# Five attentions of a two-block model: the mask's addition moved from TensorE to VectorE, the division by the sum from VectorE to GpSimd

## What is computed

```
s = q @ k.T * scale                       # 256 queries, 512 keys, 8 heads
s_local += bias                           # even: a window mask; na: relative positions, outside -1e30; mla: none
p = softmax(s, axis=-1)                   # even: a "sink" logit per head is in the sum as well
y = p @ v
```

## Time and profile before

| | |
|---|---|
| device time, median of 3 runs | 2842.94 us (2841.6 to 2846.72) |
| span of the profiled execution | 2844.0 us |
| PE busy | 2634.3 us (93%), 13686 instructions |
| VectorE busy | 807.8 us (28%), 1961 instructions |
| ScalarE busy | 453.2 us (16%), 971 instructions |
| GpSimd busy | 75.2 us (3%), 144 instructions |
| chain that ended last | PE 78%, DMA 13%, DVE 5%, issue 2%, ACT 1% |
| of it DVE L2046, DVE L2063, PE L899, PE L910 | 1%, 0%, 1%, 1% |

### The profile page before, as it was taken

One profiled execution on the slowest core, in us unless ns is written; L12 is line 12 of the kernel. 1 busy time (PEld: TensorE's weight loads), 2 busy tenths in 40 slices (PEclk: granted clock), 3 DMA queues, 4 the chain that ended last, 5 costly groups with the idle time before them and its releaser, 6 DMA issues.

```text
span 2844.0 us, 33920 instructions
## 1 busy us (share of the span) xinstructions
PE 2634.3 (93%) x13686; PEld 1826.3 (64%) x13686; DVE 807.8 (28%) x1961; ACT 453.2 (16%) x971; POOL 75.2 (3%) x144
## 2 busy tenths in 40 slices
PE   6997999889999998989998999999999899999998
PEld 2546455556667764546565666687888645787887
DVE  1344213231112252111111335415542225313002
ACT  2132002131111022000000214301000123201001
POOL 0000000000000000000000000000000000000000
PEclk9998999999999999999999999999999999999999
DMA  9795898999998739999999832243765311233430
GB/s 391 321 385 198 330 415 352 394 395 422 397 407 344 302 136 386 422 418 420 422 417 422 343 132 89 89 148 132 278 273 215 138 60 69 110 148 123 158 135 16
DMA packets 117562, 764.24 MB, mean 269 GB/s; under 512 B 12832, under 2 KB 15648, under 8 KB 34208
## 3 DMA queue, kind: packets, MB, share of 16 engines
q1 hardware_dynamic: 94400, 680.57, 59.3%
q0 software_dynamic: 20160, 73.67, 6.6%
q10 hardware_dynamic: 2848, 7.83, 0.7%
HBM read 758.61 MB, written 3.41 MB: 268 GB/s over the span
## 4 chain that ended last, share of the span: by engine, by line
PE 78%; DMA 13%; DVE 5%; issue 2%; ACT 1%; SPq 1%; ACTq 0%; DVEq 0%
PE bank L588 75%; DMA ring<-in_stream 13%; PE bank L910 1%; PE bank L899 1%; SPq L467 1%; PE bank L592 1%; DVE MX L2046 1%; DVE work L1957 1%; DVE work L2063 0%; ACT work L1520 0%; ACT A L1530 0%; DVE A L1965 0%; DVE NM L2051 0%; ACT work L1452 0%; ACT work L1448 0%
## 5 line engine op out<-in xcount | busy, mean ns | idle before, releaser
L588 PE MATMUL bank<-A,ring 128*128 128x256 f32 (+1 forms) x3088 | 714.6, 391 | 21.4 <-issue 9.6
L588 PEld LDWEIGHTS bank<-A,ring 128*128 128x128 f32 x3088 | 590.5, 192 | 142.3 <-issue 50.3
L588 PE MATMUL bank<-ring,A 128*32 128x512 f32 (+3 forms) x2304 | 397.3, 617 | 72.4 <-DMA ring<-in_stream 63.5
L588 PE MATMUL bank<-work,ring 128*128 128x256 f32 x1696 | 384.0, 384 | 5.7 <-DVE work L2556 2.1
L588 PEld LDWEIGHTS bank<-work,ring 128*128 128x128 f32 x1696 | 323.4, 191 | 56.5 <-issue 4.2
L588 PE MATMUL bank<-work 128*64 128x128 f32 (+4 forms) x2084 | 315.6, 330 | 27.9 <-ACT work L1452 6.5
L588 PEld LDWEIGHTS bank<-ring,A 128*32 128x32 f32 (+2 forms) x2304 | 124.9, 126 | 325.0 <-issue 213.0
L588 PEld LDWEIGHTS bank<-work 128*128 128x128 f32 (+2 forms) x2084 | 241.0, 172 | 79.3 <-issue 31.4
L588 PE MATMUL bank<-A,work 128*128 128x256 f32 x1280 | 287.5, 382 | 1.2 <-DVE tab_sb L1780 0.9
L588 PEld LDWEIGHTS bank<-A,work 128*128 128x128 f32 x1280 | 240.0, 190 | 55.5 <-issue 22.0
L588 PE MATMUL bank<-work,A 128*128 128x256 f32 (+2 forms) x416 | 128.0, 452 | 9.5 <-DVE X L2263 4.3
(11 more groups left out here) (290 smaller groups left out, 1518.1 us busy)
## 6 DMA issues: line engine op xcount, KB each, us to landing
ring<-in_stream SPq DMA_DIRECT2D x648, 1024.0 KB, 12.7
work<-in_stream POOLq DMA_DIRECT2D x134, 512.0 KB, 8.8
X<-in_xt ACTq DMA_DIRECT2D x1, 2048.0 KB, 14.0
spill<-work ACTq DMA_DIRECT2D x3, 512.0 KB, 9.2
work<-spill POOLq DMA_DIRECT2D x3, 512.0 KB, 5.1
tab_sb<-in_tab_a ACTq DMA_DIRECT2D x1, 1120.0 KB, 18.7
X<-in_ctx2t ACTq DMA_DIRECT2D x1, 1024.0 KB, 14.4
out<-X SPq DMA_DIRECT2D x4, 256.0 KB, 2.2
```

The lines of the kernel that those rows point to most:

```text
L588: return pay(pe.matmul(o, w, x, start=start, stop=stop, tile_position=place), tells)
```

## The change

The matmul that adds the bias (L899) goes. VectorE now takes the maximum over the last 256 keys only, and then one instruction adds the bias to the first 256 scores, in place in PSUM, and takes the maximum of these and of the one before (in even and na; in mla the maximum stays one instruction over 512). VectorE ends head t-1 with the reciprocal; the multiplication of the 128x512 weights by it is GpSimd's in all five attentions, which waits for the new semaphore `at_inv` and tells `at_pn`. The new instructions stand in GpSimd's queue between its DMAs.

```
@@ semaphores
-        at_pn, at_pv, at_y, at_es = (sem(n) for n in ("at_pn", "at_pv", "at_y", "at_es"))
+        at_inv, at_pn, at_pv, at_y, at_es = (sem(n) for n in ("at_inv", "at_pn", "at_pv", "at_y", "at_es"))
@@ GpSimd's program
+            def weigh(name, PR):
+
+                nb, u0 = ATT[name]
+                for t in range(nb * HEADS):
+                    g, b, h = u0 + t, t // HEADS, t % HEADS
+                    pool.wait_ge(at_inv, g + 1)
+                    pool.tensor_scalar(PR[:, g % 3, :], PR[:, g % 3, :], SM[:, (u0 // HEADS + b) % 2, h:h + 1], None, ALU.mult)\
+                        .then_inc(at_pn, 1)
+
+            weigh("even", PR1)
             last_taken(pool, "even_out")
...
             pool.dma_start(V2[:, 2:4, :], spill[:, 1024:2048].rearrange("p (a b) -> p a b", b=512)).then_inc(c_back, 16)
+            weigh("na0", PR2)
             pool.wait_ge(at_y, ATT["na0"][1] // HEADS + ATT["na0"][0])
...
             pool.wait_ge(c_back, 64)
+            weigh("mla0", PR2)
+            weigh("na1", PR2)
+            weigh("mla1", PR2)
@@ TensorE's program
-            def attention(name, q, k, v, PR, PT, bias=None):
+            def attention(name, q, k, v, PR, PT):
...
-                            m = mm(score_bank(name, g)[:, :], q(h, b), k(h), True, bias is None, tells=bias is None)
-                            if bias is None:
-                                m.then_inc(at_s, 1)
-                        if bias is not None:
-                            for i in range(t, t + pair):
-                                g, b, h = u0 + i, i // HEADS, i % HEADS
-                                pe.matmul(score_bank(name, g)[:, 0:T], ident, bias(h, b), start=False, stop=True)\
-                                  .then_inc(at_s, 1)
+                            mm(score_bank(name, g)[:, :], q(h, b), k(h), True, True, tells=True).then_inc(at_s, 1)
...
-                bs = [strip(FIRST[f"l{l}_bias"], h) for h in range(2)][0]
+                for h in range(2):
+                    strip(FIRST[f"l{l}_bias"], h)
@@ VectorE's program
-            def attention(name, scale, PR, y, sink=False):
+            def attention(name, scale, y, sink=False, bias=None):
...
                         dve.wait_ge(at_s, g + 1)
-                        link(dve.reduce_max(MX[:, pb, h:h + 1], score_bank(name, g)[:, :], AXX))
+                        s, top = score_bank(name, g), MX[:, pb, h:h + 1]
+                        link(dve.reduce_max(top, s[:, T:2 * T] if bias else s[:, :], AXX))
+                        if bias:
+                            link(dve.tensor_tensor_reduce(s[:, 0:T], s[:, 0:T], bias(h, b), 1.0, top, ALU.add, ALU.max, top))
...
-                        link(dve.reciprocal(total, total))
-                        dve.tensor_scalar(PR[:, g % 3, :], PR[:, g % 3, :], total, None, ALU.mult).then_inc(at_pn, 1)
+                        dve.reciprocal(total, total).then_inc(at_inv, 1)
...
-            attention("even", 1.0, PR1, lambda b: CAT[:, 0:4, b * P:(b + 1) * P], sink=True)
+            attention("even", 1.0, lambda b: CAT[:, 0:4, b * P:(b + 1) * P], sink=True,
+                      bias=lambda h, b: tab(TA, "mask", b * T, T))
...
-                attention(f"na{l}", 1.0, PR2, lambda b: YB[1][:, :, b * P:(b + 1) * P])
+                at = FIRST[f"l{l}_bias"]
+                for h in range(2):
+                    dve.wait_ge(strip_in[h][at % RING], 16 * (at // RING + 1))
+                attention(f"na{l}", 1.0, lambda b: YB[1][:, :, b * P:(b + 1) * P],
+                          bias=lambda h, b: ring[:, at % RING, (h * TB + b) * T:(h * TB + b + 1) * T])
...
-                attention(f"mla{l}", MLA_SCALE, PR2, lambda b: YB[2][:, :, b * P:(b + 1) * P])
+                attention(f"mla{l}", MLA_SCALE, lambda b: YB[2][:, :, b * P:(b + 1) * P])
```

More of the change, by code:

```diff
@@ L989, in _ @@
                       lambda kb, h: V1[:, kb, 64 * (h // 4):64 * (h // 4) + 64],
-                      PR1, PT1, bias=lambda h, b: tab(TA, "mask", b * T, T))
+                      PR1, PT1)
             pe.wait_ge(at_y, 2)
@@ L1294, in _ @@
                           lambda h: NK[64 * (h % 2):64 * (h % 2) + 64, h // 2, :],
-                          lambda kb, h: V2[:, kb, h * 64:(h + 1) * 64], PR2, PT2,
-                          bias=lambda h, b: bs[:, (h * TB + b) * T:(h * TB + b + 1) * T])
+                          lambda kb, h: V2[:, kb, h * 64:(h + 1) * 64], PR2, PT2)
                 used()
```

## The result

The change made the kernel slower: 2883.57 us (median of 4 runs, 2881.01 to 2886.87) against 2843.38 us for the kernel before on the same chip, ratio 1.0136, 95% interval 1.0124 to 1.0148. The forecast was 2840.4 us, about level, with a range of 2829 to 2855. The profiled execution has a span of 2879.1 us against 2844.0, 35.1 us more.

What follows compares the result with a forecast made beforehand. The prediction took TensorE, 78% of the chain that ended last, as the bound. Its terms for mla, na, even and clock, 6.1 - 2.0 - 7.4 + 0.8 = -2.5 us, took 2842.9 to 2840.4 us, range 2829 to 2855.

Steps and rivals of the forecast that it cites:

- L: Time from the reciprocal's end to the transposes' start: 0.56 us before, forecast 0.94, between 0.58 and 1.31.
- The Trainium skill's figure: A 512-element loop on GpSimd at 769 ns; by it L would be 1.11 and the sum 5.8 us higher.
- mla: In mla0 and mla1 L is on the chain: each pair 0.38 us longer, +6.1 us for both attentions.
- The circle of 3.03 + L: In na, scores through VectorE and GpSimd to the next scores: 3.97 us per pair, becoming the bound; -2.0 us for both.
- The forecast of -7.4: Net gain in even from removing 16 bias matmuls, limited by the DMA, less a longer end: -7.4 us.
- The 1.85 us of `mod_rows` cover L: In even, the circle has room: a head takes over 4 us and `mod_rows` hides L.
- the limit by the ring: In even, the last `mod_rows` waits for strip 28's second half, so TensorE can come only 7.2 us earlier.
- the 1.5 us for the end of even: Behind the last `mod_rows`: last scores' way to the transposes 0.7 us longer, as much again for neighbouring heads; 1.5 us.
- Clock: At na1's start TensorE's granted clock falls as at na0's; half of 1.64 us put in, +0.8 us.
- C: Rival: GpSimd at twice VectorE's time between reciprocal and transposes, L = 1.31, +10.0 us, 2853 us; chance 0.30.
- A: Rival: GpSimd nearly as quick as VectorE in mla and na, L under 0.85; 2830 us at L = 0.64; chance 0.34.
- B: The forecast itself, L between 0.85 and 1.18: gain in even, loss in mla, na about level; chance 0.36.

Runs made afterwards that it cites:

- fill_short: The changed kernel with unread matmuls in TensorE's gaps, one per gap and three at each start in na and mla, even as in fill: 2875.35 us, ratio 1.011.
- bias_only: The changed kernel with the multiplication back on VectorE, the bias still added on VectorE: 2838.76 us, ratio 0.9976.
- fill: The changed kernel with unread matmuls where TensorE waits for GpSimd, two per gap and six at the starts of na and mla: 2890.97 us, ratio 1.0155.

## Why the prediction was wrong

- **The unknown, L.** This is the term that failed: "I take 0.60 for the multiplication ... and 0.30 for the hand-over". The multiplication is 1.57 and the hand-over 0.08. The upper end, "twice that, 0.97, since two passes of this kind over the tile is the worst the nearest row suggests", was no bound: it was the duration of another engine with a factor that no row carried. The two errors in the hand-over and the multiplication have opposite signs, but the second is four times the first. The forecast used a DMA issue for the hand-over the earlier trace rows, 0.30 us; a compute instruction of GpSimd followed in 0.08.
- **The Trainium skill's figure.** 769 ns for 512 elements (GPSIMD Engine Reference, section 3.1) was on the right side, and half of what was measured. The runs decide: 1562 ns for 512 columns.
- **mla.** The mechanism was right to 0.01 us: the pair is 4.30 + L - 0.56. With L = 1.70 the 8 pairs are 9.1 us per attention. Measured were 10.0 and 11.0. From the first to the last maximum it is 38.60 us against 29.83, and from there to the end of the last transposes 4.93 against 3.80, which is 1.14 for L again: 9.9 for mla0. In mla1 that tail is 6.27, at a clock that fell (4.93 in fill_short, where it didn't).
- **na.** The circle of 3.03 + L was right in each step, and so was the addition (0.58 forecast, 0.49 + 0.07 on the chain). Only L is off. The tail was not as forecast, one multiplication longer: 6.3 and 7.8 us were lost where 7 x 0.56 + 1.14 = 5.1 follows from L. From the last maximum to the end of the last transposes it is 6.32 us against 3.79 before and 4.11 in bias_only, so GpSimd adds 2.2 there and not 1.14. The chain at na0's end shows why:

```profile
1737.05 1.57 POOL work L547
...
1739.85 0.78 ACT work L1595 x2
1740.92 1.57 POOL work L547
```

Behind the last maximum (1736.87) two of GpSimd's multiplications lie on it, one after another. The last head's exponentials stand behind the copy of the transposed weights of two heads before in ScalarE's order, so they wait for the first multiplication, and the second waits for them.
- **even.** The forecast of -7.4 (by its own terms, 7.2 + 1.9 - 1.5, it is -7.6) would have been too small without GpSimd: at even's end bias_only is 11.3 us earlier, 9.5 of it gained in even. With GpSimd it was 1.3, and 0.6 of it in even. "The 1.85 us of `mod_rows` cover L" holds where they stand: the limit by the ring gave 6.0 of its 7.2 us. Behind the last of them it fails. The forecast had that end 0.4 us shorter (1.5 - 1.9), and it became 4.7 longer, with L = 1.70 on the chain twice and a clock that fell. fill puts 5.9 us on the clock. The failed step is the 1.5 us for the end of even.
- **Clock.** +0.8 was forecast. The granted clock fell at even's end and at the start of na0, mla0, na1 and mla1. By fill and fill_short this is worth 2.5 to 5.9 us in even and 2.4 us in mla0, na1 and mla1 together; in na0 the filler gained nothing, so what the clock costs there is not shown. These are differences between single profiles.
- **Rivals.** C named the place, the mechanism and the side, and stopped at L = 1.31 because of the factor of two. The slope of 34 us per us of L puts the forecast at 2840.4 + 34 x 0.76 = 2866 for L = 1.70. In the profiled spans that is a change of +23.3, and +35.1 was measured: 5.9 of the difference are in even (0.0 against -5.9), 3.9 in na (14.1 against 10.2) and 2.7 in mla (21.0 against 18.3), which are the tails and the clock (for which 0.8 was in). The medians lie another 5 us apart, more than the spans. A and B fell with L.
- **Costing nothing.** VectorE's wait for the bias strip and the DMAs behind GpSimd's multiplications show up nowhere on the chain, as forecast.

What stays open: how much of even's gain reaches the end of the program. The identical stretch behind it varied by 9.6 us between profiles, and the time before it by 4.2, more than the effect. For the same reason the clock's share of the whole time stays open; at even's own end it is shown.

## What to carry to other kernels

Before moving an operation to an engine, ask whether its result is waited for on the circle that sets the pace. If it is, the price is the other engine's latency for every turn, whatever the share of busy time, and a bound for that latency needs a row of that engine doing that kind of work. Where no row exists, a factor on another engine's duration is a guess and belongs in a much wider range.

If an engine's latency is on such a circle, a deeper pipeline is worth more than a faster place for the operation: one more buffer and one head's delay brought 1.8% with GpSimd (1.0136 to 0.9952) and 0.35% in the kernel before. An operation that leaves TensorE waiting can cost twice, by the wait and by the clock after it.

## What was unexpected of the hardware

- GpSimd's multiplication by a per-partition scalar, f32 in SBUF: 1562 ns for 128x512 and 922 ns for 128x256, against VectorE's 487 and 353 (the latter beside GpSimd). Its start after VectorE's reciprocal took 0.08 us.
- The same GpSimd instruction over 256 columns takes 0.16 us more when VectorE multiplies in SBUF beside it, and VectorE's did not get longer (353 ns; a 128x256 multiplication of SBUF by a scalar elsewhere in the same kernel took 350).
- Two f32 products of 64 rows by 512 columns, on different halves and into different banks, took 1.13 us together, one alone 1.12, and two on the same half and into the same bank 1.98.
